# A seventh gate/up slot in the rows of h of a hybrid decoder step with 32 experts

## What is computed

```python
h = h + concat([pool_out, ssd_out]) @ w_out            # two mixers, 512 columns each; w_out 1024 x 1024
u = rmsnorm(h, norm_ffn)
# router: best group of 4, in it the best 2 of 8 experts, for each token
# expert e: (silu(u @ w_gate[e]) * (u @ w_up[e])) @ w_down[e]   w_gate, w_up 1024 x 256; w_down 256 x 1024
h = h + moe(u)                                         # weighted sum of the two experts of a token
h = h + sigmoid(rmsnorm(h, norm_ple) @ ple_gate_w + ple_gate_b) * (p @ ple_proj_w)
y = rmsnorm(h, norm_final)
```

## Time and profile before

| | us |
|---|---|
| median of 3 runs (lowest, highest) | 543.52 (539.91, 545.23) |
| the profiled execution's own time | 540.01 |
| its span in the profile | 538.2 |
| TensorE busy | 503.0 (93%) |
| VectorE busy | 214.2 (40%) |
| ScalarE busy | 154.3 (29%) |
| DMA | 145.71 MB, mean 271 GB/s over the span |
| read from DRAM, written | 141.24 MB, 15.24 MB |

### The profile page before, as it was taken

One profiled execution on the slowest core, in us unless ns is written; L12 is line 12 of the kernel. 1 busy time (PEld: TensorE's weight loads), 2 busy tenths in 40 slices (PEclk: granted clock), 3 DMA queues, 4 the chain that ended last, 5 costly groups with the idle time before them and its releaser, 6 DMA issues.

```text
span 538.2 us, 7829 instructions
## 1 busy us (share of the span) xinstructions
PE 503.0 (93%) x3122; PEld 308.0 (57%) x3122; DVE 214.2 (40%) x509; ACT 154.3 (29%) x318; POOL 111.6 (21%) x169
## 2 busy tenths in 40 slices
PE   5999999999999999799999999988888989999993
PEld 4888886888545555455555555544444543444453
DVE  2187696523034556662222222212111111579344
ACT  1436263112524121112222222221121224454123
POOL 0300058994201002101111211110111112031001
PEclk9999999999999999899999999998988999999997
DMA  8993000604469905999999999999999996941012
GB/s 308 399 327 110 1 1 7 229 1 95 156 242 395 381 5 181 404 406 411 416 414 417 412 419 414 414 418 414 417 416 416 416 411 252 373 170 40 2 40 79
DMA packets 41577, 145.71 MB, mean 271 GB/s; under 512 B 14620, under 2 KB 15260, under 8 KB 32420
## 3 DMA queue, kind: packets, MB, share of 16 engines
q1 hardware_dynamic: 33956, 131.77, 62.3%
q0 software_dynamic: 5152, 8.71, 4.4%
q10 hardware_dynamic: 2432, 4.71, 2.3%
HBM read 141.24 MB, written 15.24 MB: 291 GB/s over the span
## 4 chain that ended last, share of the span: by engine, by line
PE 71%; DMA 12%; SPq 8%; DVE 6%; ACT 1%; issue 1%; POOLq 0%; ACTq 0%; POOL 0%; DVEq 0%
PE PS L1047 13%; PE PS L833 10%; PE PS L1161 10%; PE PS L639 10%; DMA mem<-in_exp_w_up 9%; PE PS L1068 7%; PE PS L610 6%; PE PS L599 5%; SPq L493 3%; SPq L497 2%; SPq L491 2%; DVE mem L1720 1%; PE PS L897 1%; DMA mem<-choice_rows 1%; DMA mem<-in_w_a 1%
## 5 line engine op out<-in xcount | busy, mean ns | idle before, releaser
L1047 PE MATMUL PS<-mem 128*64 128x256 f32 x512 | 122.1, 393 | 13.2 <-DMA mem<-in_exp_w_up 13.0
L1048 PE MATMUL PS<-mem 128*64 128x256 f32 x512 | 122.2, 394 | 0.0
L1047 PEld LDWEIGHTS PS<-mem 128*64 128x64 f32 x512 | 69.6, 141 | 49.5 <-DMA mem<-in_exp_w_up 10.6
L639 PE MATMUL PS<-mem 128*128 128x260 f32 x320 | 73.3, 386 | 0.0
L1048 PEld LDWEIGHTS PS<-mem 128*64 128x64 f32 x512 | 69.7, 141 | 0.0
L639 PEld LDWEIGHTS PS<-mem 128*128 128x128 f32 x320 | 60.0, 190 | 10.4 <-issue 1.5
L2021 DVE TENSOR_TENSOR mem<-PS,mem 64x256 f32<-64x256 f32 x32 | 13.7, 427 | 128.6 <-ACT mem L1364 128.4
L1068 PE MATMUL PS<-mem 128*64 128x512 f32 x256 | 62.0, 605 | 1.1 <-ACT mem L1370 0.7
L833 PE MATMUL PS<-mem 128*128 128x512 f32 x128 | 56.6, 596 | 0.0
L1161 PE MATMUL PS<-mem 128*128 128x512 f32 (+1 forms) x144 | 56.0, 547 | 0.0
L1364 ACT ACTIVATE mem<-PS 64x256 f32<-64x256 f32 x32 | 12.0, 375 | 113.3 <-PE PS L1048 113.3
(11 more groups left out here) (290 smaller groups left out, 550.4 us busy)
## 6 DMA issues: line engine op xcount, KB each, us to landing
mem<-in_exp_w_down SPq DMA_DIRECT2D x32, 1024.0 KB, 23.8
mem<-in_exp_w_gate SPq DMA_DIRECT2D x32, 1024.0 KB, 21.5
mem<-in_exp_w_up SPq DMA_DIRECT2D x32, 1024.0 KB, 23.5
mem<-in_w_out SPq DMA_DIRECT2D x2, 2048.0 KB, 7.3
mem<-in_ple_gate_w SPq DMA_DIRECT2D x2, 2048.0 KB, 16.6
mem<-choice_rows SPq DMA_DIRECT2D x4, 1024.0 KB, 13.4
mem<-in_x_prompt SPq DMA_DIRECT2D x4, 512.0 KB, 14.5
mem<-in_w_v SPq DMA_DIRECT2D x1, 2048.0 KB, 24.9
```

Source lines behind the costliest of these rows:

```text
L639: ins = pe.matmul(PS[b + h][:, 0:HALF], w[:, k, :], aT[:, k, h * HALF:(h + 1) * HALF], start=(k == 0), stop=(k == KT - 1))
L1047: pe.matmul(PS[0][0:S, 0:FF], rows_k, gu[slot][:, k, :], start=(k == 0), stop=(k == KT - 1))
L1048: ins = pe.matmul(PS[1][S:2 * S, 0:FF], rows_k, gu[slot][:, KT + k, :], start=(k == 0), stop=(k == KT - 1))
```

## The change

The rows of the prompt in `h1` are stored to a new tensor in DRAM, `h_rows`, one tile at a time as soon as they are complete (`store_h`, 0.5 MiB each), and read back in the tail, where `combine` waits for them as well. The 16 KiB per partition that they take hold a seventh gate/up slot in between: its gate half lies over tiles 0 and 1, its up half over tiles 2 and 3. So block 6's gate weights wait for the store, the transposes and ScalarE's reading of the first two tiles, and its up weights for the same of all tiles and for `select`.

The output projection is put into another order on TensorE: the k 0 to 3 of the last two tiles are done first, which frees the first half of `w_out` and `v`. A signal there lets SyncE load block 4's gate and up weights and block 6's down weights. The four gate/up slots of the loop and those under the tail's weights change places, and with them the addresses of `w_ple`, `Yg[4]` and `yout`. In the written-out blocks the gate and up weights of b + 7 are issued ahead of the down weights of b + 6; the last of the latter is issued after the loop over b. Four semaphores are merged into two (`s_tri_G_done`, `s_BC_eE_done`), and `s_gn_done` becomes `s_gn_part_done`, whose third count is the new signal; the lines on these are left out of the diff.

```diff
@@ -51,12 +51,12 @@
 NBX = NBT - NE
 HEAD = 28
 HP = HEAD // 2
-NGU, NDN = 6, 7
+NGU, NDN = 7, 7
 EPS = 1e-6
 
 
 def gu_slot(b):
-    return (b + 2) % NGU if b < HEAD else (b - HEAD) % U
+    return b % NGU if b < HEAD else (b - HEAD) % U
 
 
 def dn_slot(b):
@@ -175,7 +175,7 @@
         xg = [at(R_dn, 4, TOK), at(R_z, 4, TOK)]
         rdiag = at(R_dn + 5 * TOK, NT, P)
         rstd_b = at(R_dn + 4 * TOK, TOK)
-        gu = [at(r, 2 * KT, FF) for r in (R_gu + 2 * GU, R_gu + 3 * GU, R_xc, R_xc + GU, R_gu, R_gu + GU)]
+        gu = [at(r, 2 * KT, FF) for r in (R_xc, R_xc + GU, R_gu, R_gu + GU, R_gu + 2 * GU, R_gu + 3 * GU, R_x)]
         dn = [at(r, 2, D) for r in (R_dn, R_dn + DN, R_samp + 1024, R_v, R_d3, R_aT, R_aT + 4 * TOK)]
         assert R_row - R_xc >= 2 * GU and R_xc - R_aT >= GU + DN
         w_out = at(R_gu + 2 * GU, KT, D)
@@ -224,7 +224,7 @@
         pp = [at(R_dn + t * D, D) for t in range(4)] + [at(R_d3, D)]
         w_pp = at(R_aT, 2, D)
         pT = at(R_aT + 2 * D, 2, TOK)
-        w_ple = [at(R_gu + h * KT * 512, KT, 512) for h in range(2)]
+        w_ple = [at(R_gu + (2 + h) * GU, KT, 512) for h in range(2)]
         bfin = at(R_samp + 1024, D)
         bple = at(R_samp + 2048, D)
 
@@ -238,8 +238,8 @@
         actT = at(R_actT, 2, 2 * S)
         ysb = at(R_row, 2, D)
 
-        Yg = [at(R_xc + 2 * t * D, 2, D) for t in range(4)] + [at(R_gu + 2 * GU, 2, D)]
-        yout = at(R_gu + 2 * GU + 2 * D, NT, D)
+        Yg = [at(R_xc + 2 * t * D, 2, D) for t in range(4)] + [at(R_gu, 2, D)]
+        yout = at(R_gu + 2 * D, NT, D)
         sm = [R_small]
 
         def small(*shape, rows=P):
@@ -330,6 +330,7 @@
 
         u_dram = nc.dram_tensor("u_rows", (TOK, D), F32).ap()
         y_dram = nc.dram_tensor("choice_rows", (2 * TOK, D), F32).ap()
+        h_dram = nc.dram_tensor("h_rows", (SEQ, D), F32).ap()
 
 
...
@@ -487,11 +487,17 @@
                              a["state_ssm"][0, :, 2 * t:2 * t + 2].rearrange("b h p n -> (h p) b n")
                              ).then_inc(ld_hs, 16)
 
-            def load_gate_up(slot, src_e):
+            def load_gate(slot, src_e):
                 sp.dma_start(gu[slot][:, 0:KT, :], a["exp_w_gate"][src_e].rearrange("a (p k) f -> p (a k) f", p=P)
                              ).then_inc(w_full[slot], 16)
+
+            def load_up(slot, src_e):
                 sp.dma_start(gu[slot][:, KT:2 * KT, :], a["exp_w_up"][src_e].rearrange("a (p k) f -> p (a k) f", p=P)
                              ).then_inc(w_full[slot], 16)
+
+            def load_gate_up(slot, src_e):
+                load_gate(slot, src_e)
+                load_up(slot, src_e)
 
             def load_down(slot, src_e):
                 sp.dma_start(dn[slot], a["exp_w_down"][src_e].rearrange("a (k p) n -> p (a k) n", p=P)
...
@@ -534,11 +540,31 @@
             load_down(dn_slot(2), bass.ds(2, 1))
             load_down(dn_slot(4), bass.ds(4, 1))
 
+            def store_h(i):
+                t = ORDER[i]
+                sp.wait_ge(s_outp_out, 2 * i + 2)
+                sp.dma_start(h_dram[t * P:(t + 1) * P, :], h1[:, t, :]).then_inc(st_h, 16)
+
+            store_h(0)
+            store_h(1)
+            sp.wait_ge(s_gn_part_done, 3)
+            load_gate_up(gu_slot(4), bass.ds(4, 1))
+            load_down(dn_slot(6), bass.ds(6, 1))
+            sp.wait_ge(s_uTr_done, 4)
+            sp.wait_ge(s_u_ready, 2)
+            sp.wait_ge(st_h, 32)
+            load_gate(gu_slot(6), bass.ds(6, 1))
+            store_h(3)
             sp.wait_ge(s_outp_done, 2 * NT)
-            for b in (4, 5):
-                load_gate_up(gu_slot(b), bass.ds(b, 1))
-            for b in (5, 6):
-                load_down(dn_slot(b), bass.ds(b, 1))
+            load_gate_up(gu_slot(5), bass.ds(5, 1))
+            load_down(dn_slot(5), bass.ds(5, 1))
+            store_h(4)
+
+            sp.wait_ge(s_uTr_done, 2 * NT)
+            sp.wait_ge(s_u_ready, NT)
+            sp.wait_ge(s_sel_done, 2)
+            sp.wait_ge(st_h, 64)
+            load_up(gu_slot(6), bass.ds(6, 1))
 
             for b in range(HEAD - NGU):
                 sp.wait_ge(s_up_done, b + 1)
@@ -546,6 +572,8 @@
                 if b >= 1:
                     sp.wait_ge(s_Y_ready, b)
                     load_down(dn_slot(b + 6), bass.ds(b + 6, 1))
+            sp.wait_ge(s_Y_ready, HEAD - NGU)
+            load_down(dn_slot(HEAD - 1), bass.ds(HEAD - 1, 1))
 
             sp.wait_ge(s_rt_ready, 1)
             n = sp.value_load(nloop[0:1, 0:1], min_val=(NE - HEAD) // U, max_val=(NB - HEAD) // U)
@@ -563,6 +591,9 @@
             sp.dma_start(pT, a["pT"]).then_inc(ld_wo1_pp, 16)
             ple_rows = a["ple_gate_w"][0].rearrange("(k p) n -> p k n", p=P)
             sp.dma_start(w_ple[0], ple_rows[:, :, 0:512]).then_inc(ld_wple[0], 16)
+            for t in TAIL:
+                if t < 4:
+                    sp.dma_start(h1[:, t, :], h_dram[t * P:(t + 1) * P, :]).then_inc(yg_full[t], 16)
             sp.wait_ge(s_Y_ready, n * U + (HEAD - 1))
 
             for q in range(2):
...
@@ -858,7 +889,7 @@
                 for h in range(2):
                     ins = pe.matmul(PS[4 + 2 * g + h][:, 0:HALF], ones, zs[:, 2 * g, h * HALF:(h + 1) * HALF],
                                     start=True, stop=True)
-                ins.then_inc(s_gn_done, 1)
+                ins.then_inc(s_gn_part_done, 1)
             pe.wait_ge(s_inproj_out, len(COLS) - NA)
             outproj_part(1, 0, 4)
             pe.wait_ge(ld_wo1_pp, 16)
@@ -990,26 +1021,29 @@
             h_rows(1, 0)
             h_rows(1, 1)
             pe.wait_ge(s_outp_out, 4)
-            out_half(3, 0, 0, KT)
+            outproj_part(3, 0, 4)
             route(1)
             h_rows(2, 0)
             h_rows(2, 1)
             count(0)
-            out_half(3, 1, 0, KT)
+            pe.wait_ge(s_outp_out, 6)
+            outproj_part(4, 0, 4).then_inc(s_gn_part_done, 1)
             route(2)
             count(1)
-            pe.wait_ge(s_outp_out, 6)
-            out_half(4, 0, 0, KT)
+            out_half(3, 0, 4, KT)
+            out_half(3, 1, 4, KT)
+            out_half(4, 0, 4, 6)
             h_rows(3, 0)
             h_rows(3, 1)
             count(2)
-            out_half(4, 1, 0, 2)
+            out_half(4, 0, 6, KT)
             route(3)
+            out_half(4, 1, 4, 5)
             h_rows(4, 0)
             first_pair_slots()
-            out_half(4, 1, 2, 6)
+            out_half(4, 1, 5, 7)
             count(3)
-            out_half(4, 1, 6, KT)
+            out_half(4, 1, 7, KT)
             h_rows(4, 1)
             route(4)
             pe.wait_ge(s_outp_out, 9)
...
@@ -1904,21 +1938,21 @@
             take_h(1, 1)
             take_logits(0)
             choose(0)
-            residual(3, 0)
             take_logits(1)
             take_h(2, 0)
             take_h(2, 1)
             choose(1)
             rank(0)
             place(0)
-            residual(3, 1)
             take_logits(2)
             choose(2)
             rank(1)
             place(1)
-            residual(4, 0)
+            residual(3, 0)
+            residual(3, 1)
             take_h(3, 0)
             take_h(3, 1)
+            residual(4, 0)
             rank(2)
             place(2)
             take_logits(3)
@@ -2051,7 +2085,7 @@
             def combine(i):
                 t = TAIL[i]
                 R = ROWS[t]
-                dve.wait_ge(yg_full[t], 16)
+                dve.wait_ge(yg_full[t], 32 if t < 4 else 16)
                 for h in range(2):
                     hh = slice(h * 512, (h + 1) * 512)
                     half = h1[0:R, t, hh]
```

29 lines of the change are left out of this document (14 added, 15 removed).

## The result

| | before | with the change |
|---|---|---|
| median (lowest to highest), us | 542.4 (539.26 to 545.23) | 544.64 (542.32 to 547.63) |
| ratio to before, 95% interval | 1 | 1.0064 (1.0047 to 1.0080) |
| span of the profiled execution, us | 538.2 | 543.1 |
| DMA, MB | 145.71 | 149.90 |

The forecast was 541.8 us, 1.7 us less than before; by the ratio it came out 3.5 us more (0.64% of 542, interval 2.5 to 4.3). The two medians of the table are only 2.2 us apart and the means 2.7, so it is sure that the change makes the kernel slower, and less sure by how much. The measured time lies in the range given, on the other side of "no change" than the forecast. It is the outcome that the forecast had as rival 3, with an addition that it did not have.

A forecast was written before the change was run, and what follows sets the result against it. The weight stream was taken to bound the kernel; -5.05 - 1.0 + 1.0 + 1.7 = -3.35 us at the last weights and +1.7 in the tail made -1.65, so 541.8 us from a median of 543.5, range 537.5 to 546.0.

The forecast's parts named there:

- rival 3: Tail: the scatter takes turns with the h rows, landing after 8.0 us instead of 3.2; 545 us, chance 0.16.
- What bounds the kernel: Expert blocks: from about 342 us the weight stream sets the end; what counts is when the last up weights land.
- the sum: Whole kernel: -3.35 us at the last weights, +1.7 us in the tail, together -1.65 us.
- (a): Expert stream: a seventh gate/up slot leaves two fewer transfers, 2.10 MB, behind block 0's gate/up; -5.05 us.
- (b): Stream at 226.90 us: leftover backlog gone, -1.0 us (0 to -1.6); starting anew costs +1.0 us (0.5 to 2).
- (c): Idle stretch, 190 to 203 us: loading block 4's and half of block 6's weights early makes (a) possible; nothing by itself.
- (d): Output projection: the new order makes the last residual and the stream's start later, +1.7 us (0 to +3.5).
- (e): Tail: reading h back, 2.10 MB ahead of the choice rows, delays the last scatter; +1.7 us (0 to +4.8).
- rival 4: Front: a longer pause drops TensorE's clock for select, first transposes and block 0; 544 to 549.5 us, chance 0.06.
- Rival 2: Front and tail: the order costs nothing and the h rows are hidden; 537.5 to 538.5 us, chance 0.24.
- Rival 5: Stream: block 6's up half comes after block 0 is done, so (a) halves; about +1, 544.5 us, chance 0.04.

The follow-up runs named there:

- a1: The changed kernel without the four reads of h in the tail, for its time alone; 0.9939 of before, median 538.54 us.
- a3: The changed kernel with the old order of the output projection, block 4's loads and block 6's down weights behind it; 1.0105 of before, median 547.48 us.
- b2: The kernel before with only the new order of TensorE and VectorE in the output projection, six slots, loads as before; 1.0017 of before, median 542.80 us.
- c1: The changed kernel with three of the four reads of h moved behind the last scatter, each behind its tile's choice rows; 1.0015 of before, median 543.14 us.
- c3: The changed kernel with c1's late reads and choose(3) moved ahead of take_h(4, 0) on VectorE; 1.0010 of before, median 541.93 us.
- e1: c3 with VectorE's combine(3) and combine(4), and ScalarE's norms of these tiles, moved later in the tail; 0.9924 of before, median 537.72 us.

## Why the prediction went wrong, by its own steps

- **What bounds the kernel** (the weight stream, and the last up weights as the point that decides): right. a1 shows that the change is a gain when nothing is lost behind them, 3.3 us (2.0 to 4.6). That this meets the sum's 3.35 so closely is luck: in the profile the last weights came 1.7 us earlier, not 3.35, and TensorE waited 12.1 us for `in_exp_w_up` where about 9.5 was forecast (13.0 before).
- **(a) seventh slot, -5.05 us:** right in its bytes; with **(b)** it came to -4.4 us in the mean of the profiles and -3.4 in the changed kernel's. The credit for a backlog (-1.0) was not there, since the changed kernel had as much left over, and the restart was 1.5 us instead of 1.0 in that profile.
- **(c) early loads as what makes (a) possible:** right; without them 2.1 us of the 4.4 remain, and a3 is 1.0% slower than before.
- **(d) the order, +1.7 us:** right to 0.1 us in the trace, at the last residual and at block 0. In the time of b2 it is 0.9 us (0 to 2.0).
- **(e) the reads of h, +1.7 us (0 to 4.8): the step that failed.** It measured +6.8 us, 6.6 by the tails of the profiles. Two mistakes in it. The landing: I let the scatter land when the h rows are done, 4.8 us after its issue. It did land when the queue had emptied, but I had let the queue empty at 410 GB/s, and it ran down at 209 and then 74 GB/s, so the landing came after 7.36 us, near the median row of 8.0 us. And the bound itself was too low: I priced the wait of TensorE behind it as if it were only its length. At the same zero slack on which I rested, a wait of 3.0 us is followed here by matmuls at half the clock, 3 us more. I had looked at the clock for the front (rival 4) and not for the tail, where the wait was the longer one.
- **The sum:** -3.35 + 6.8 = +3.45 is no test of the rest, since the 6.8 is itself the measured 3.5 less the -3.3 of a1. The profiles give the parts by themselves: -3.4 between the blocks, +1.7 up to block 0, +6.6 in the tail, together the 4.9 us by which the two profiled executions differ (span 538.2 and 543.1). With 1.7 us for (e) these parts would have come to no change. So the forecast's gain was lost in the stream (1.7 us short of -5.05), and the slowdown is all of (e).
- **The rivals:** rival 3 is what came (0.16). That it said 545 and the median was 544.64 is partly luck: it started from 543.5, where the kernel before has 542.4 in more executions, its price of 4.8 us, for the scatter alone, left out the clock, and its stream was 1.7 us too good. The point it gave, a landing of 6.5 us or more, decided. Rival 2 was refuted in both halves, (d) is not 0 in the trace and the reads are not hidden. Rival 4 did not occur: the second `select` took 2.94 us, 3.00 before. Rival 5 did not occur: block 6's up half went out 4 us ahead of the end of block 0's gate/up.

## What to carry to other kernels

A small transfer on which everything waits (here a scatter of at most 128 rows) has the price of what other queues hold when it moves: bulk loads belong behind it, even where the bytes are free in the sum. A wait of TensorE in a stage without slack costs its length and can cost slower matmuls behind it (waits of 3.04 and 3.50 us did, one of 3.07 us did not), so a bound for such a wait needs a row of the clock as well as a row of the wait. And when data is moved to land later, the order of the engine that takes it has to move with it: without that move c1 and c3 gained 0.5% on the changed kernel, with it e1 gained 1.4%.

## What the runs showed of the hardware

The same 128x512 product pair took 1.72 us at the granted clock 1.00 and 3.41 us at 0.51 behind an idle TensorE of 3.0 us; behind one of 3.07 us in c1 the clock stayed at 1.00. The last scatter landed in 3.17 to 3.69 us in the eight kernels with at most 0.5 MiB of h behind the tail's first weights and in 6.97 to 7.46 us in the six with 2 MiB there; nothing lay in between. In the changed kernel the last 4 us of the queue moved 209 and 74 GB/s, where a full one moves 415, and the scatter landed when it was empty. And the start of block 0 moved by 2.6 us among kernels with the same code up to there: the granted clock fell to the lower level for a few microseconds in 211 to 226 us, once or twice, and not at the same place.
